# One of the first four modulation tiles moves from VectorE to TensorE, and the narrow projections start on half of the chunks

## What is computed

```python
cond = jax.nn.silu(c)
for layer in range(DEPTH):
    mod = cond @ ada_w[layer] + ada_b[layer]
    sh1, sc1, g1, sh2, sc2, g2 = jnp.split(mod, 6, axis=-1)
    h = modulate(rms_norm(x, mix_norm[layer]), sh1, sc1)
    ...

def modulate(h, shift, scale):
    return h * (1.0 + scale[:, None, :]) + shift[:, None, :]
```

## Time and profile before

| | |
|---|---|
| median of 3 runs | 1827.93 us (1827.38 to 1832.44) |
| the profiled execution | 1831.7 us, of which the span of instructions is 1830.4 us |
| mean granted TensorE clock | 0.959 |
| PE busy | 1649.4 us (90%) |
| DVE busy | 682.5 us (37%) |
| DMA | 577.35 MB, mean 315 GB/s |

### The profile page before, as it was taken

How to read it: one execution, slowest core, us unless ns; L and a number is a source line. 1 busy time by engine, 2 the same in 40 slices (tenths; PEclk the granted TensorE clock), 3 DMA queues, 4 the chain that set the end, 5 groups by cost and what they waited for, 6 DMA issues and landing times.

```text
span 1830.4 us, 21289 instructions
## 1 busy us (share of the span) xinstructions
PE 1649.4 (90%) x9047; PEld 1008.6 (55%) x9047; DVE 682.5 (37%) x1296; ACT 387.5 (21%) x664; POOL 36.7 (2%) x39
## 2 busy tenths in 40 slices
PE   4989999999999999999999978899788887888877
PEld 3766899998689999887533322233222222222223
DVE  6668477745967556592210101011010110100102
ACT  2222444433434435360100000000000000000001
POOL 0101000000000000200010000000000000000000
PEclk8999999999999999999899989999899998999999
DMA  9655367736657544234599999999999999999996
GB/s 395 254 226 195 143 236 300 253 139 267 236 198 256 200 166 180 100 126 147 217 418 412 430 430 417 431 428 432 430 429 429 430 429 431 428 426 431 428 430 265
DMA packets 43551, 577.35 MB, mean 315 GB/s; under 512 B 4785, under 2 KB 5954, under 8 KB 7234
## 3 DMA queue, kind: packets, MB, share of 16 engines
q1 hardware_dynamic: 43458, 576.00, 76.9%
HBM read 574.93 MB, written 1.05 MB: 315 GB/s over the span
## 4 chain that ended last, share of the span: by engine, by line
PE 69%; DMA 23%; DVE 6%; ACT 1%; issue 1%; SPq 0%; DVEq 0%; ACTq 0%
DMA RING_T<-in_w_up 21%; PE P L1133 19%; PE P L459 9%; PE P L1158 5%; PE P L798 4%; PE P L796 4%; PE P L797 4%; PE P L817 2%; PE P L816 2%; PE P L815 2%; PE P L1111 2%; DVE RING_T L1770 2%; PE P L1175 2%; PE P L468 2%; DMA RING_T<-in_ada_w 1%; PE P L935 1%
## 5 line engine op out<-in xcount | busy, mean ns | idle before, releaser
L1133 PE MATMUL P<-RING_T,SCR 128*34 128x512 f32 x1008 | 481.7, 634 | 115.3 <-DMA RING_T<-in_w_up 115.3
L1134 PE MATMUL P<-RING_T,SCR 128*34 128x512 f32 x992 | 475.6, 636 | 0.0
L1133 PEld LDWEIGHTS P<-RING_T,SCR 128*34 128x34 f32 x1008 | 114.3, 118 | 430.7 <-issue 430.1
L2350 DVE TENSOR_TENSOR SCR<-P,SCR 34x512 f32<-34x512 f32 x64 | 44.4, 693 | 592.7 <-ACT SCR L1653 592.7
L1158 PE MATMUL P<-RING_T,SCR 128*34 128x512 f32 x512 | 228.1, 594 | 9.3 <-DMA RING_T<-in_w_down 9.2
L1159 PE MATMUL P<-RING_T,SCR 128*34 128x512 f32 x512 | 228.1, 594 | 0.0
L796 PE MATMUL P<-SCF 128*128 128x256 f32 x640 | 181.1, 283 | 0.0
L797 PE MATMUL P<-SCF 128*128 128x256 f32 x640 | 181.1, 283 | 0.0
L798 PE MATMUL P<-SCF 128*128 128x256 f32 x640 | 181.1, 283 | 0.0
L1653 ACT ACTIVATE SCR<-P 34x512 f32<-34x512 f32 x64 | 37.8, 591 | 617.9 <-PE P L1134 617.9
L1158 PEld LDWEIGHTS P<-RING_T,SCR 128*34 128x34 f32 x512 | 53.6, 111 | 154.0 <-issue 126.8
(11 more groups left out here) (317 smaller groups left out, 2133.6 us busy)
## 6 DMA issues: line engine op xcount, KB each, us to landing
RING_T<-in_w_gate SPq DMA_DIRECT2D x63, 2048.0 KB, 16.7
RING_T<-in_w_down SPq DMA_DIRECT2D x63, 2048.0 KB, 13.0
RING_T<-in_w_up SPq DMA_DIRECT2D x62, 2048.0 KB, 12.1
RING_T<-in_ada_w SPq DMA_DIRECT2D x24, 2048.0 KB, 11.6
RING_T<-in_ffn_w SPq DMA_DIRECT2D x22, 2048.0 KB, 8.1
RING_T<-in_ffn_w SPq DMA_DIRECT2D x22, 1024.0 KB, 4.9
RING_T<-in_ab_w_in SPq DMA_DIRECT2D x7, 2048.0 KB, 17.5
RING_T<-in_w_in SPq DMA_DIRECT2D x6, 2048.0 KB, 8.3
```

What stands on the lines that cost most here:

```text
L1133: pe.matmul(u.t[0:CAP, :], xs, wg.v(KC, 512)[:, c, :], start=c == 0, stop=c == KC - 1)
L1134: ins = pe.matmul(u.t[64:64 + CAP, :], xs, wu.v(KC, 512)[:, c, :], start=c == 0, stop=c == KC - 1)
```

## The change

Tile 3 of layer 0 is stored in another layout (input features on the partitions) and multiplied on TensorE, with a new column form `C8` of silu(c) as the one moving column. It leaves VectorE's list. VectorE adds its bias out of PSUM, between the third and the fourth group of tile 1. `SA` is made in two halves. All eight products x times 1/rms are now VectorE's. The 18 dummy matmuls are gone, and so is the wait on `mod`. The narrow projections run as: 40 columns on chunks 0 to 3, 128 columns on chunks 0 to 3, then the same on chunks 4 to 7. SP issues one more DMA, `C8`, second of all.

```diff
+ADA_PE = (0, 3)
+ADAS = [x[1:] for x in LOADS if x[0] == "ada" and x[1:] != ADA_PE]

 pe_ab:
+    w = ring["ada", *ADA_PE]
+    u = pe_bank(nc, k, "mod_pe")
+    pe.wait_ge(s["cond"], 2)
+    pe.wait_ge(w.sem, w.n)
+    for g in range(4):
+        for c in range(KC):
+            ins = pe.matmul(u.t[:, g:g + 1], w.v(KC, 512)[:, c, g * 128:(g + 1) * 128], k.C8[:, c:c + 1], start=c == 0, stop=c == KC - 1)
+    ins.then_inc(u.full, 1)
+    w.left = (u.full, u.n)
     pe.wait_ge(s["narrow"], 16)
-    pe.wait_ge(s["mod"], 2)
-    pe_busy(nc, k, u, 12, 128)
-    for c in range(KC):
-        if c == 4:
-            pe_busy(nc, k, u2, 6, 128)
-        pe.wait_ge(s["hn"], HN["mix0"] + c + 1)
-        ins = pe.matmul(u.t[0:40, 0:T], v.WN[:, c, 0:40], k.HX[:, c, :], start=c == 0, stop=c == KC - 1)
-    ins.then_inc(u.full, 1)
-    u = u2
-    for c in range(KC):
-        ins = pe.matmul(u.t[:, 0:T], v.WN[:, c, 40:168], k.HX[:, c, :], start=c == 0, stop=c == KC - 1)
-    ins.then_inc(u.full, 1)
+    for half in range(2):
+        for c in range(4 * half, 4 * half + 4):
+            pe.wait_ge(s["hn"], HN["mix0"] + c + 1)
+            ins = pe.matmul(u.t[0:40, 0:T], v.WN[:, c, 0:40], k.HX[:, c, :], start=c == 0, stop=c == KC - 1)
+        if half:
+            ins.then_inc(u.full, 1)
+        for c in range(4 * half, 4 * half + 4):
+            ins = pe.matmul(u2.t[:, 0:T], v.WN[:, c, 40:168], k.HX[:, c, :], start=c == 0, stop=c == KC - 1)
+    ins.then_inc(u2.full, 1)

 act_ab:
+    act.activation(k.C8[:, :], k.C8[:, :], ACT.Silu).then_inc(s["cond"], 1)
...
-    act.wait_ge(s["sa"], 1)
     for c in range(KC):
         if c % 4 == 0:
+            act.wait_ge(s["sa"], 1 + c // 4)
             act.wait_ge(s["mod"], ADA_AT[0, c // 4] + 1)
-            act.wait_ge(s["xr_p" if c else "xr"], 4)
+        act.wait_ge(s["xr"], c + 1)

 dve_ab:
-    for c in range(4):
+    for c in range(KC):
         dve.tensor_tensor(k.H[:, c, M:L], k.X[:, c, M:L], k.RS[:, 0, 0:T], ALU.mult).then_inc(s["xr"], 1)
+    dve.wait_ge(s["mod"], 1)
+    adjusted(0)
     dve_ada_sums(nc, k, 1)
     dve_mod(nc, k, 1)
-    dve_adjusted(nc, k, 0, 0)
-    for n in (2, 3):
-        dve_ada_sums(nc, k, n)
-        dve_mod(nc, k, n)
+    dve_ada_sums(nc, k, 2, 0, 3)
+    u = P["mod_pe"]
+    dve.wait_ge(u.full, u.n)
+    dve.tensor_tensor(k.MOD[:, 0, 12:16], u.t[:, 0:4], k.vv("ada_b", 12, 16), ALU.add).then_inc(u.taken, 1)
+    dve.wait_ge(u.taken, u.done)
+    adjusted(1)
+    dve_ada_sums(nc, k, 2, 3, 4)
+    dve_mod(nc, k, 2)

 pool_ab:
-    pool.wait_ge(s["rs"], rms_done("mix0"))
-    for c in range(4, KC):
-        pool.tensor_tensor(k.H[:, c, M:L], k.X[:, c, M:L], k.RS[:, 0, 0:T], ALU.mult).then_inc(s["xr_p"], 1)

 sync_program:
     sp.dma_start(k.CB[:, :], A["c"].broadcast_to([128, D])).then_inc(s["cond_in"], 16)
+    sp.dma_start(k.C8[:, :], A["c_cols"]).then_inc(s["cond_in"], 16)
```

More of the change, by code:

```diff
@@ L95 @@
     LOADS += [(x, _e, i) for i in range(4) for x in "gu"] + [("d", _e, i) for i in range(4)]
-ADAS = [x[1:] for x in LOADS if x[0] == "ada"]
+ADA_PE = (0, 3)
+ADAS = [x[1:] for x in LOADS if x[0] == "ada" and x[1:] != ADA_PE]
 ADA_AT = {x: n for n, x in enumerate(ADAS)}
@@ L131, with sa_done @@
 NUNIT = len(UNITS)
+def sa_done(layer, part):
+    return 2 * layer + part + 2
 class Use:
@@ L240 @@
     "vecs", "cond_in", "ones_in", "consts", "x", "pos", "narrow", "small", "gup", "later", "poolw", "ex0", "ex1", "ex2", "last0", "last1", "last2", "last3", "out",
-    "cond", "ada", "mod", "xr", "xr_p", "sa", "square", "squares", "ln", "rs", "hs", "hn",
+    "cond", "ada", "mod", "xr", "sa", "square", "squares", "ln", "rs", "hs", "hn",
     "angle", "trig", "g1one", "iwt", "gate_a", "gate_d", "decay_a", "decay_d", "cosm", "rope", "qeke", "kdqd", "atzero", "at", "relu", "score",
@@ L281, in __init__ @@
         self.CB = sbt("CB", [128, D], F32)
+        self.C8 = sbt("C8", [128, KC], F32)
         self.RS = sbt("RS", [128, 4, L], F32)
@@ L1251, in act_shift @@
 def act_shift(nc, k, name, layer):
-    nc.scalar.wait_ge(k.sem["sa"], 2 * layer + 1)
+    nc.scalar.wait_ge(k.sem["sa"], sa_done(layer, 0))
     for c in range(KC):
@@ L1262, in act_ab @@
     act_table(nc, SET_SILU)
-    act.wait_ge(s["cond_in"], 16)
+    act.wait_ge(s["cond_in"], 32)
     act.activation(k.CB[:, :], k.CB[:, :], ACT.Silu).then_inc(s["cond"], 1)
+    act.activation(k.C8[:, :], k.C8[:, :], ACT.Silu).then_inc(s["cond"], 1)
     act_table(nc, SET_EXP)
@@ L1441, in act_ffn @@
     name = ("ffn0", "ffn1")[layer]
-    act.wait_ge(s["sa"], 2 * layer + 2)
+    act.wait_ge(s["sa"], sa_done(layer, 1))
     act_stat(nc, k, name, M)
@@ L1757, in dve_rope, with dve_ada_sums @@
     nc.vector.tensor_tensor(dst, dst, tmp, ALU.add).then_inc(k.sem[sem], 1)
-def dve_ada_sums(nc, k, n):
+def dve_ada_sums(nc, k, n, a=0, b=4):
     layer, i = ADAS[n]
@@ L1767, in dve_ada_sums @@
         nc.vector.wait_ge(k.sem["cond"], 1)
-    for g in range(4):
+    for g in range(a, b):
         src = w.v(4, D)[:, g, :]
@@ L1795, in dve_adjusted @@
                                    in1=w, op0=ALU.add, op1=ALU.mult).then_inc(k.sem["sa"], 1)
-    nc.vector.wait_ge(k.sem["sa"], 2 * layer + part + 1)
+    nc.vector.wait_ge(k.sem["sa"], sa_done(layer, part))
 def dve_scaled(nc, k, name, sa):
@@ L1843, in dve_ab, with adjusted @@
     dve.wait_ge(s["rs"], rms_done("mix0"))
-    for c in range(4):
+    for c in range(KC):
         dve.tensor_tensor(k.H[:, c, M:L], k.X[:, c, M:L], k.RS[:, 0, 0:T], ALU.mult).then_inc(s["xr"], 1)
+    def adjusted(h):
+        a, b = 4 * h, 4 * h + 4
+        dve.scalar_tensor_tensor(out=k.SA[:, 0, a:b], in0=k.MOD[:, 0, 8 + a:8 + b], scalar=1.0, in1=k.vv("mix_norm", a, b),
+                                 op0=ALU.add, op1=ALU.mult).then_inc(s["sa"], 1)
+    dve.wait_ge(s["mod"], 1)
+    adjusted(0)
     dve_ada_sums(nc, k, 1)
     dve_mod(nc, k, 1)
-    dve_adjusted(nc, k, 0, 0)
-    for n in (2, 3):
-        dve_ada_sums(nc, k, n)
-        dve_mod(nc, k, n)
+    dve_ada_sums(nc, k, 2, 0, 3)
[6 more added lines that the diff above has]
+    dve_mod(nc, k, 2)
     pf, kk, an = v.AP, v.AK, v.AN
@@ L2717 @@
     narrow = np.concatenate([w[:, 1024:1040], np.zeros((D, 16), np.float32), w[:, 3664:3672], keys, keys], 1)
+    ada = g["ada_w"].reshape(2, D, 12, 4, 128).transpose(0, 2, 4, 3, 1).reshape(2, 12, 128, SLOT).copy()
+    ada[ADA_PE] = columns(g["ada_w"][ADA_PE[0]], (512 * ADA_PE[1],))[0]
     arrays = {
@@ L2725 @@
         "gup": np.concatenate([g["gla_gate_up"][0], g["gla_gate_b"]], 0),
-        "c": g["c"], "ada_w": g["ada_w"].reshape(2, D, 12, 4, 128).transpose(0, 2, 4, 3, 1).reshape(2, 12, 128, SLOT),
+        "c": g["c"], "c_cols": cols(g["c"]), "ada_w": ada,
         "ab_w_in": columns(w, (3088, 0, 512, 1552, 2064, 2576, 1040)), "ab_w_out": columns(g["ab_w_out"][0], (0, 512)),
```

## The result

The changed kernel took 1835.43 us (median of 12 runs, 1830.74 to 1843.87), the kernel before 1829.22 us (median of 12 runs beside it, 1826.31 to 1837.22). The ratio is 1.0028 with a 95% interval of 1.0015 to 1.0041: **about 5 us slower** (6.2 by the medians), where 3 us faster was forecast. The profiled execution has a span of 1835.1 us.

A forecast was written before the change was run, and what follows sets the result against it. The prediction took the start of `iq` to bound the kernel, behind VectorE's then TensorE's chain. `iq` at 42.8 instead of 45.47 gains 2.7: 1827.9 - 2.7 = 1825.2, said as 1825 us, range 1819.5 to 1830.

The forecast's parts named there:

- The bound and the chain at the start: First 45 us: VectorE's chain up to 38 us, then TensorE's; what counts is how much earlier `iq` starts than 45.47.
- The new work: Tile 3 on TensorE: 64 one-column pairs, 6 at full clock, 58 at 0.22 us, from 18.6 to 32.0.
- the first rival: Clock stays up or returns during the one-column work: `iq` at 39.1, a gain of 6.3, 1821.6 us; chance 0.22.
- VectorE and ScalarE: At the start, VectorE's shorter list lets ScalarE's first half start at 28.3 and its second at 33.8 instead of 37.94.
- The clock's return: TensorE's full clock returns 4.8 us after the narrow projections start at 32.0; `iq` at 42.8, a gain of 2.7.
- The rest: Side effects (product off GpSimd, extra silu, wait for C8, extra PSUM bank) were put at no cost.
- I expect a shift of `iq` to go through to the end: Behind `iq`, its earlier start, a gain of 2.7 us, was to be kept to the kernel's end.
- The third: Rival: without the dummies the clock doesn't return before `iq`; some 4 us lost, 1832 us; chance 0.06.
- the distance from `iq` to the end: Sign in the profile after: this stays 1785 us; if grown by `iq`'s gain, the shift did not go through.

The follow-up runs named there:

- e2: The changed kernel with C8 laid into the first 8 columns of CL, so the ring lies where it did before; ratio to the kernel before 0.9981.
- e1: The kernel before with one unused allocation of 32 bytes per partition behind CB, ahead of the ring; ratio 1.0031 (1.0018 to 1.0045).
- e13: The changed kernel with C8 allocated as 512 bytes per partition; median 1829.12 us, ratio to the kernel before 0.9997 (0.9983 to 1.0012).
- e12: e2 with C8's DMA issued behind tile 2 and its silu computed behind the statistic; ratio to the kernel before 0.9993 (0.9978 to 1.0008).
- e4: The kernel before with only the new 4 KB input and its DMA, data unused, nothing in SBUF moved; ratio 0.9987 (0.9975 to 1.0000).
- e7: e2 with 19 dummy matmuls ahead of the new one-column work and 16 behind it; ratio to the kernel before 0.9989 (0.9974 to 1.0003).
- e11: e12 with 19 dummy matmuls ahead of the new one-column work, none behind; ratio to the kernel before 0.9967 (0.9954 to 0.9979).

## Why the prediction was wrong

- **The bound and the chain at the start**: right. `iq` decides, and its shift was kept at 134 us and through to the expert stage (848.6 us from `iq` to there, before 849.7). Over all profiles that distance is 846.4 to 850.2 us, so one pair of profiles shows it to a few us only.
- **The new work**: right. 0.22 a pair was forecast and 0.215 measured; it began 0.6 us late and ended at 33.0 instead of 32.0 (18.6, 0.8 and 12.8 add up to 32.2). The price came from the 10 pairs at half clock in rows 5 and the clock from L1111, and both rows served. The advice of the Trainium skill (TensorE: Matmul & The Clock Gate, section "Why this matters for your kernels") to keep TensorE busy, which would have made the first rival the forecast, did not bring the full clock with one-column matmuls (0.50 throughout 22 to 33 us).
- **VectorE and ScalarE**: right to 0.7 and 1.0 us (28.3 and 33.8 forecast, 28.98 and 34.84 measured). Most of it is the loads: tile 0 was used from 24.03, not 23.4.
- **The clock's return**: 4.8 us taken, 3.3 measured in this execution and 5.5 in e2's. `iq` came at 43.3 (forecast 42.8, a gain of 2.2 and not 2.7), which is near in part by luck: the late start and the early return of the clock cancel. The five changed kernels without dummies and with `C8`'s DMA second range over 42.1 to 44.6.
- **"The rest"**: here it failed. The part went through what the extra silu, the extra bank and GpSimd's freed time cost, and found zero. It left out the allocation that the change adds to SBUF: no term of the sum stands for `C8`'s 32 bytes. That term is 5.7 us by itself (e1, 3.3 to 8.2), and it arises almost wholly in the expert stage, which begins some 850 us behind `iq`. With it the step "I expect a shift of `iq` to go through to the end" failed for the changed kernel: 3.2 us of lead at 892 us became 4.7 us of lag.
- **The rivals**: none was this one. The third, on the slower side, had the dummies' absence as its mechanism, and the clock came back in 3.3 us. The range ended at 1830, below all 12 runs (the fastest 1830.74).
- **How to tell it**: the test that I had named, the distance from `iq` to the end (1785 forecast), pointed to it: it is 1835.1 - 43.3 = 1791.8. By itself it settles little, as it is 1791.7 in e13 as well, where the packets are short and 542 long ones fell into the execution.

Settled by runs: the pad alone costs what the change lost (e1), and the change without the shift does not lose it (e2, e12, e13). Whether the change then gains at the end is not settled. The ratios are 0.9981, 0.9993 and 0.9997; e2's interval alone lies below 1, and e4, which has nothing to gain, came out at 0.9987. The profiles do show `iq` 1 to 3 us earlier.

## What to carry to other kernels

Count allocations among the edits: one that stands ahead of a buffer that is streamed into moves it, and in a stage that waits for DMA 4 ns more on packets of 611 cost 0.3% of this kernel. When the time changes and the edited stretch does not explain it, compare the same packets or instructions in an untouched stage, and then try the edit's side effects alone, the allocation first, since a pad of unused bytes is a one-line experiment. The 64 pairs with one moving column did not keep TensorE's clock up (e7, e11), and so the wide matmuls behind them began at half clock.

## What was not expected of the hardware

A 16 KB packet into SBUF took 611 ns where the ring started at 96 modulo 256 bytes of the allocations, and 612 to 621 ns (means 613.8 to 615.1) at the other places tried, in e1 with the source unchanged. Yet at the same shifted places all of them took 611 ns between 12 and 24 us, in the changed kernel and in e1. And TensorE's clock fell to 1.2 GHz 4.4 us into a gapless run of one-column matmuls that had started at 2.4 GHz (e7).
